# Second block of a three-block model: rope table, rope, keys' norm and values' transposes moved beside the product that makes queries, keys and values

## The reference, cut to what matters

```python
qkv = h @ w_qkv                                    # h: normed tokens, 512 x 1024
q = rope_slice(rms_norm(q, q_gain), cos, sin, 0)   # 16 heads of 64, norm per head, 16 of 64 features turned
k = rope_slice(rms_norm(k, k_gain), cos, sin, 0)   # 4 heads of 64
sc = q @ k.T * 64 ** -0.5                          # band: |query - key| <= 128
m = max(max(sc), sink)
p = exp(sc - m); p = p / (sum(p) + exp(sink - m))
o = p @ v
```

## Time and profile before

| | us |
|---|---|
| median of 3 runs (lowest, highest) | 3731.3 (3728.52, 3731.86) |
| the profiled execution's own time | 3727.72 |
| its span | 3725.9 |
| TensorE busy | 3421.0 (92%) |
| VectorE busy | 2036.8 (55%) |
| ScalarE busy | 1451.3 (39%) |
| GpSimd busy | 737.9 (20%) |

### The profile page before, as it was taken

One profiled execution on the slowest core, in us unless ns is written; L12 is line 12 of the kernel. 1 busy time (PEld: TensorE's weight loads), 2 busy tenths in 40 slices (PEclk: granted clock), 3 DMA queues, 4 the chain that ended last, 5 costly groups with the idle time before them and its releaser, 6 DMA issues. The chain is left out here.

```text
span 3725.9 us, 46521 instructions
## 1 busy us (share of the span) xinstructions
PE 3421.0 (92%) x18648; PEld 2713.6 (73%) x18648; DVE 2036.8 (55%) x2943; ACT 1451.3 (39%) x2400; POOL 737.9 (20%) x506
## 2 busy tenths in 40 slices
PE   8988999999879999977999997997999999989998
PEld 6656788877457888753688775766888888768787
DVE  6565534356555434535557375536666666546554
ACT  6435322344354222322544242445454444334232
POOL 1000302120002212201011012415444444301100
PEclk9889999999789999986999997998999999989999
DMA  4101322222012222210033232442000000022222
GB/s 145 34 1 60 105 96 96 95 80 68 1 40 85 96 94 93 96 39 0 19 107 111 74 102 71 160 163 65 21 24 24 24 24 32 4 83 96 96 91 79
DMA packets 82293, 260.48 MB, mean 70 GB/s; under 512 B 9632, under 2 KB 13216, under 8 KB 81696
## 3 DMA queue, kind: packets, MB, share of 16 engines
q1 hardware_dynamic: 71424, 236.02, 19.0%
q10 hardware_dynamic: 10656, 21.50, 1.5%
HBM read 236.51 MB, written 20.97 MB: 69 GB/s over the span
## 5 line engine op out<-in xcount | busy, mean ns | idle before, releaser
L1512 DVE TENSOR_TENSOR mlp_w_lo<-mlp_ring,mlp_w_hi 128x1024 fp32r<-128x1024 f32 (+1 forms) x211 | 251.3, 1192 | 601.4 <-ACT mlp_w_hi L1492 601.2
L1492 ACT ACTIVATE mlp_w_hi<-mlp_ring 128x1024 fp32r<-128x1024 f32 (+1 forms) x211 | 213.2, 1011 | 689.8 <-PE ps L1470 683.9
L1512 DVE TENSOR_TENSOR ffn_w_lo<-ffn_ring,ffn_w_hi 128x1024 fp32r<-128x1024 f32 (+3 forms) x172 | 222.4, 1293 | 469.8 <-ACT ffn_w_hi L1492 469.8
L1492 ACT ACTIVATE ffn_w_hi<-ffn_ring 128x1024 fp32r<-128x1024 f32 (+3 forms) x172 | 187.3, 1089 | 509.9 <-PE ps L1470 504.9
L1469 PE MATMUL ps<-mlp_more_parts,mlp_w_hi 128*128 128x512 f32 x952 | 374.0, 393 | 0.0
L1468 PE MATMUL ps<-mlp_more_parts,mlp_w_hi 128*128 128x512 f32 x760 | 306.5, 403 | 38.4 <-DVE mlp_w_lo L1512 24.1
L1468 PE MATMUL ps<-tiles_parts,mlp_w_hi 128*128 128x512 f32 x832 | 331.0, 398 | 5.7 <-issue 5.7
L1468 PE MATMUL ps<-ffn_x_parts,ffn_w_hi 128*128 128x512 f32 x792 | 312.3, 394 | 22.7 <-DVE ffn_x_parts L2202 20.9
L1470 PE MATMUL ps<-tiles_parts,mlp_w_lo 128*128 128x512 f32 x832 | 328.7, 395 | 0.0
L1469 PE MATMUL ps<-ffn_x_parts,ffn_w_hi 128*128 128x512 f32 x792 | 310.1, 392 | 0.0
L1470 PE MATMUL ps<-ffn_x_parts,ffn_w_lo 128*128 128x512 f32 x792 | 309.9, 391 | 0.0
(11 more groups left out here) (486 smaller groups left out, 7057.7 us busy)
## 6 DMA issues: line engine op xcount, KB each, us to landing
ffn_ring<-in_w_ffn_up SPq DMA_DIRECT2D x88, 512.0 KB, 3.3
mlp_ring<-in_w_up SPq DMA_DIRECT2D x64, 512.0 KB, 3.3
mlp_ring<-in_w_down SPq DMA_DIRECT2D x64, 512.0 KB, 3.3
rwkv_keep<-ffn_ring ACTq DMA_DIRECT2D x64, 256.0 KB, 2.3
sq<-rwkv_keep SPq DMA_DIRECT2D x64, 256.0 KB, 2.9
ffn_ring<-in_w_ffn_down SPq DMA_DIRECT2D x16, 768.0 KB, 4.3
in_ring<-in_w_in SPq DMA_DIRECT2D x22, 512.0 KB, 3.3
mlp_ring<-in_w_in SPq DMA_DIRECT2D x22, 512.0 KB, 3.3
```

The source lines that it names most:

```text
L1492: nc.scalar.activation(w.w_hi[:, n % SPLIT, 0:width], w.ring[:, n % RING, 0:width], ACT.Copy).then_inc(s["w_hi_ready"], 1)
L1512: nc.vector.tensor_tensor(w.w_lo[:, n % SPLIT, 0:width], w.ring[:, n % RING, 0:width], w.w_hi[:, n % SPLIT, 0:width].bitcast(F32), ALU.sub ...
```

## The change

The stages of `second_block` before the attention go. Their work is done in a new class, `Attended`, whose programs are woven into the last two products of the `mlp1` chain: the rope table's 12 VectorE steps beside the gate's tiles 4, 5 and 6; rope of keys and queries, the keys' norm, the doubled keys and the values' transposes beside and behind the 12 tiles of the product. The product's tile order becomes keys (0, 1), queries (2 to 9), values (10, 11). The queries are not normed: the rotation uses a matrix that is multiplied with the gain, and the queries' rstd per token and head goes into the exponential's scale and into the maximum, by one more instruction per group. The chain `mlp1` uses 5 banks for output tiles, so that bank 5 is free for the sums of squares. GpSimd has no part in it any more. The positions and the bands are loaded by SP within the chain, behind the load for gate tile 4, after a wait for all slots before the gate; SP then waits until the bands have landed.

```diff
+def qkv_product(nc, m, a, normed, y, prep):
+    def on_dve(dve, s, lin, t):
+        if t == 0:
+            normed.invert(dve, s)
+        if t < lin.tiles:
+            dve.wait_ge(s["slots_used"], lin.used(t))
+            nc.vector.tensor_tensor(y[:, t, :], m.ps[:, lin.bank(t), :], m.rstd[:], ALU.mult).then_inc(s["bank_free"][lin.bank(t)], 1)
+        prep.beside("dve", dve, s, t if t < lin.tiles else math.inf)
+    def on_act(act, s, lin, t):
+        if t == 0:
+            normed.root(act, s)
+        prep.beside("act", act, s, t if t < lin.tiles else math.inf)
+    def beside(t):
+        def emit(pe, s):
+            if t == 0:
+                normed.sums(pe, s)
+            prep.beside("pe", pe, s, t if t < QKV_TILES - 1 else math.inf)
+        return emit
...
@@ gated_embedding, on_dve @@
+        if prep and t < DT:
+            prep.beside("dve", dve, s, t - DT)
@@ class Attended @@
+    def tables_in(self, a, gate):
+        def emit(sp, s):
+            sp.wait_ge(s["slots_used"], gate.slot)
+            sp.dma_start(self.positions, a["positions2"]).then_inc(s["q_positions_in"], 16)
+            sp.dma_start(self.bands, a["bands2"]).then_inc(s["q_bands_in"], 16)
+            sp.wait_ge(s["q_bands_in"], 16)
+        return emit
+    def act(self, act, s):
+        yield 0
+        act.wait_ge(s["r_angles"], 1)
+        for t in (m.sin, m.cos):
+            nc.scalar.activation(t[:], t[:], ACT.Sin).then_inc(s["r_tables"], 1)
+        for n in range(10):
+            yield n + 1
+            self.there(act, s, n)
...
+            nc.scalar.activation(into, tile, ACT.Square).then_inc(s["b_squared"], 1)
+            if n == 3:
+                act.wait_ge(s["b_k_sums"], 1)
+                nc.scalar.activation(self.k_root, m.ps[:, 7, 0:4 * NT], ACT.Sqrt, ...).then_inc(s["b_k_root"], 1)
+            if n == 6:
+                act.wait_ge(s["b_k_turned"], 1)
+                nc.scalar.activation(self.k_rows, m.ps[0:4, 7, :], ACT.Copy).then_inc(s["b_k_rows"], 1)
+        yield 12
+        act.wait_ge(s["b_sums"], 8)
+        nc.scalar.activation(self.root, m.ps[:, 5, 0:16 * NT], ACT.Sqrt, ...).then_inc(s["b_root"], 1)
+        for g in range(2):
+            act.wait_ge(s["b_v_turned"], g + 1)
+            nc.scalar.activation(self.v_tok[:, g, ...], m.ps[:, 6 + g, :], ACT.Copy).then_inc(s["b_v_ready"], 1)
+    def pe(self, pe, s):
+        for beat in range(1, 12):
+            yield beat
+            n = beat - 1
+            if n < 10:
+                self.there(pe, s, n)
+                if n == 0:
+                    pe.wait_ge(s["b_ready"], 3)
+                else:
+                    pe.wait_ge(s["b_sine"], n)
...
+                nc.tensor.matmul(m.ps[:, 6, :], rot, tile, start=True, stop=True).then_inc(s["b_rotated"], 1)
+            if beat == 3:
+                pe.wait_ge(s["b_squared"], 2)
...             # 8 matmuls of keys' squares, 2 columns each, into bank 7 -> b_k_sums
+            if beat == 6:
+                pe.wait_ge(s["b_k_rstd"], 1)
...             # 4 transposes of 4 columns into bank 7 -> b_k_turned
+            if beat in (8, 10):
+                g = (beat - 8) // 2
+                if g == 0:
+                    pe.wait_ge(s["b_k_rows"], 1)
+                else:
+                    pe.wait_ge(s["b_doubled"], 4)
+                nc.tensor.matmul(m.ps[:, 7, :], m.rows_out[0:4, g * P:(g + 1) * P], self.k_rows, ...).then_inc(s["b_spread"], 1)
+            if beat >= 4:
+                i = beat - 4
+                pe.wait_ge(s["b_squared"], i + 3)
...             # 4 matmuls of a query tile's squares, 2 columns each, into bank 5 -> b_sums
+        for g in range(2):
+            self.there(pe, s, QV + g)
+            if g == 0:
+                pe.wait_ge(s["b_sine"], 10)
+            else:
+                pe.wait_ge(s["b_doubled"], 8)
...         # 4 transposes of a value tile into bank 6 + g -> b_v_turned
+    def dve(self, dve, s):
+        yield -DT
...     # rotation matrices times gains, negative sinks -> b_ready
+        yield -4
+        dve.wait_ge(s["q_positions_in"], 16)
+        next(angles)                       # 3 steps
+        yield -3
+        next(angles)                       # 5 steps
+        yield -2
+        next(angles)                       # 4 steps
+        dve.sem_inc(s["r_angles"], 1)
+        for n in range(10):
+            yield n + 1
+            self.there(dve, s, n)
+            nc.vector.scalar_tensor_tensor(out=self.cosine[:, n % 2, :], in0=tile, scalar=gain, in1=m.cos[:], ...)
+            dve.wait_ge(s["b_rotated"], n + 1)
+            nc.vector.tensor_tensor(self.sine[:, n % 2, :], m.ps[:, 6, :], m.sin[:], ALU.mult).then_inc(s["b_sine"], 1)
...
+            nc.vector.tensor_tensor(tile, self.cosine[:, n % 2, :], self.sine[:, n % 2, :], ALU.add).then_inc(s["b_roped"], 1)
+            if n == 4:
+                yield 5.5
+                dve.wait_ge(s["b_k_root"], 1)
+                nc.vector.reciprocal(self.k_root, self.k_root).then_inc(s["b_k_rstd"], 1)
+            if n >= 8:
+                g = n - 8
+                yield 9.2 + 2 * g
+                dve.wait_ge(s["b_spread"], g + 1)
...             # 4 products of 64x512, keys times bank 7, into the doubled keys -> b_doubled
+        yield 12
+        dve.wait_ge(s["b_root"], 1)
+        nc.vector.reciprocal(self.root, self.root).then_inc(s["b_rstd"], 1)
...     # two scalings of 128x64: POS_Q and NEG_Q
@@ band_attention @@
-                    nc.vector.scalar_tensor_tensor(out=st(n, NEG_MAX), in0=st(n, MAX), scalar=-HD ** -0.5, in1=by_bank(neg_sink, n), ...)
+                    nc.vector.tensor_tensor(st(n, SCALED_MAX), st(n, MAX), scale_of(NEG_Q, n), ALU.mult)
+                    dve.wait_ge(s["scaled_max"], n + 1)
+                    nc.vector.tensor_tensor(st(n, NEG_MAX), st(n, SCALED_MAX), by_bank(f.neg_sink, n), ALU.min)
-                            nc.scalar.activation(p[...], scores_of(n)[:, y, slot, :], ACT.Exp, scale=HD ** -0.5, ...)
+                            nc.scalar.activation(p[...], scores_of(n)[:, y, slot, :], ACT.Exp, scale=scale_of(POS_Q, n)[:, y, slot:slot + 1], ...)
```

More of the change, by code:

```diff
@@ L175, in rope_table @@
     magic = 12582912.0
[L176 to L212, removed]
@@ new lines, in rope_angles @@
+    for part in (high, mid, low):
+        step(nc.vector.scalar_tensor_tensor(out=sin[:], in0=turns, scalar=-part, in1=sin[:], op0=ALU.mult, op1=ALU.add))
+    yield
+    step(nc.vector.tensor_scalar(turns, sin[:], np.pi / 2, -two_pi, ALU.is_gt, ALU.mult))
+    step(nc.vector.scalar_tensor_tensor(out=cos[:], in0=sin[:], scalar=np.pi / 2, in1=turns, op0=ALU.add, op1=ALU.add))
+    for t in (sin, cos):
+        step(nc.vector.tensor_scalar(t[:], t[:], 3.1415925, -3.1415925, ALU.min, ALU.max))
+    yield
@@ L314, in by_bank, with scale_of @@
             return columns[:, g * 8 + h:g * 8 + h + G].rearrange("p (s y) -> p y s", y=2)
+        def scale_of(which, n):
+            return by_bank(f.scales[:, which, groups[n][2], :], n)
         def st(n, which):
@@ L523, in dve @@
     def dve(self, dve, s):
[L524 to L530 removed]
+        nc, m = self.nc, self.m
         done = [0]
@@ L1418, in chain @@
     for lin in linears:
-        lin.slot = len(slots)
+        lin.slot, lin.banks = len(slots), banks
         for t in range(lin.tiles):
@@ L1438, in steps @@
                     yield lin, lin.tiles + more
-    with stage(nc, name, f"loaded*{RING}", "w_hi_ready", "w_lo_ready", "slots_used", "small_done", f"bank_free*{BANKS}", *signals) as (block, s):
+    with stage(nc, name, f"loaded*{RING}", "w_hi_ready", "w_lo_ready", "slots_used", "small_done", f"bank_free*{banks}", *signals) as (block, s):
         @block.sync
@@ L1457, in _ @@
                 tile = lin.place[t]
-                if part == 0 and tile >= BANKS:
-                    pe.wait_ge(s["bank_free"][tile % BANKS], tile // BANKS)
+                if part == 0 and tile >= banks:
+                    pe.wait_ge(s["bank_free"][tile % banks], tile // banks)
                 pe.wait_ge(s["w_lo_ready"], n + 1)
-                into = m.ps[:, tile % BANKS, :]
+                into = m.ps[:, tile % banks, :]
                 for k in range(lin.ks):
@@ L1772, in dve, with gated_embedding @@
                                                 op0=ALU.mult, op1=ALU.mult).then_inc(s["post_scaled"], 1)
-def gated_embedding(nc, m, a, layer, normed, e, then):
+def gated_embedding(nc, m, a, layer, normed, e, then, prep=None):
     sq = m.sq
@@ L1850, in in_projection @@
     return [first, Linear(a["w_in"], layer * NIN, NIN, DT, normed.rhs, normed.arrived, 1, {t: beside(t) for t in range(NIN)}, act, dve, last=2)]
-def scaled_product(nc, m, weights, tiles, normed, y):
+def qkv_product(nc, m, a, normed, y, prep):
     def on_dve(dve, s, lin, t):
```

257 lines of the change are left out of this document (128 added, 129 removed).

## The result

The changed kernel took 3677.3 us, the median of four executions (3675.3 to 3681.6), against 3731.2 for the kernel before in the same job (3728.5 to 3731.9): a ratio of 0.9866, 95% interval 0.9852 to 0.9881. The forecast was 3679, range 3667 to 3692.

A forecast was written before the change was run, and what follows sets the result against it. TensorE, busy 92% of the span, was taken as the bound. Terms -84.2 + 19.4 + 4.6 + 3.0 + 3.3 + 1.6 = -52.3 us, from a median of 3731.3, gave 3679 us, range 3667 to 3692.

The forecast's parts named there:

- removed, net: Between the second block's product and its attention: 90.6 us of stages go, 6.4 us stay, 84.2 us saved.
- TensorE work in the product: Inside the product: rotations, sums of squares, transposes and spreads put between the tiles' matmuls add 19.4 us.
- two waits: In the product, TensorE idles behind tiles 6 and 10 waiting for VectorE, 2.3 us each, 4.6 us; bounds 0 and 8.
- clock behind them: In the product, matmuls after each idle time run at the low clock: 1.5 us each, 3.0 us; bounds 0 and 4.
- angles beside the gate: At the gate's last tiles, rope-table steps put VectorE behind and delay normed tiles: 3.3 us; bounds 0 and 8.
- attention: In attention, one more small peak instruction costs 0.2 us in eight groups: 1.6 us; bounds -3 and 6.4.
- the product (28.5 for 25 to 28): Sign: from first tile's end to last tile's end the product grows by 25 to 28 us.
- the barrier (1.14 for at most 1): Sign at the attention stage's start: a barrier with more than 1 us would show the prediction wrong; 0.82 was counted.
- angles collide: Rival: at gate tiles 5 and 6 GpSimd and VectorE hold each other up, 8 us instead of 3.3; 3684; chance 0.12.
- Stage's start: From the end of the product's last matmul to the first score's matmul: 6.4 us, with four doubled products at 2.6.
- the banks: Five banks instead of six in the second layer's chain cost nothing; rival that they make it slower than before, chance 0.02.
- SP's two DMAs: Before the load of gate tile 5, SP's two loads and its wait cost nothing, as loads are issued 22 us ahead.

The follow-up runs named there:

- waits gone: Kernel after with the keys' roots inverted one step earlier and both spreads and the doubled keys one beat earlier: 3670.7 us, ratio 0.9846 to the kernel before.

## Why the prediction was right, and where its terms were not

The steps as the prediction put them, with what the stretch shows (after less before, us):

```
step                            forecast   measured   from
removed, net                     -84.2      -83.4     E-S 90.64 and 7.25
TensorE work in the product      +19.4      +19.8     gaps behind tiles 1 to 10, waits gone
two waits                         +4.6       +5.0     2.36 and 2.66
clock behind them                 +3.0       +3.7     the rest of T1-E: 28.5 - 19.8 - 5.0
angles beside the gate            +3.3       +5.5     N-T1, 36.51 and 30.97
attention                         +1.6       +2.4     S-O (2.8 between the means)
sum                              -52.3      -47.0     N-F
```

The mechanism held at every step, and the two large terms, 84.2 removed and 19.4 added, came out within 0.8 us, because both were read from rows of the same work elsewhere in the trace. The sum was 5.3 us too good, and all six terms erred to that side. That the medians nevertheless fell by 53.9 us in the first job (and by 49.2 in the second) is the 3420 to 3432 us of unchanged code: before's median alone was 3723.1 to 3731.2 over the jobs. With the measured steps the prediction's own sum would have given 3731.3 - 47.0 = 3684. That 3679 stood so near 3677.3 is luck. Two of the prediction's signs came out beyond their bounds, as told above: the product (28.5 for 25 to 28) and the barrier (1.14 for at most 1).

**Angles (3.3, measured 5.5).** The step took the collision as a wash: "perhaps two" steps meet GpSimd and the tail saves as much. By the rows above more met it: L1580 took 2.20 instead of 1.23, L185 1.50 instead of 0.43, L186 1.63 instead of 0.69, and the three of L183 3.12 instead of 2.14, 4.0 us in all against the 3.0 that the tail saved. The Trainium skill (SBUF — State Buffer, "Who interferes with whom") says that a VectorE instruction with two SBUF inputs, or in a two-port mode, contends with a GpSimd one that reads SBUF, and that the shared ports are held for a whole instruction. The trace agrees with it, L185's 1.50 against 0.43. So the wash was short by 1.0, and it left out the clock behind it. 4.5 us reach the end of tile 0, and 1.0 more comes behind it, where TensorE's sums of squares ran at the low clock. The rival "angles collide" had the cause right and the size too large (8): the truth lay about half way between it and the forecast.

**Attention (1.6, measured 2.4 to 2.8).** The peak's second instruction was sized well (1.6, measured 1.8), in part by luck: in the row of waits from which it was counted only 0.9 shows (4.2 with it, 3.3 without). The failed sentence is that a scale from a table costs nothing because "the instruction stays" and ScalarE waits there anyway. It costs 1.6 us, 90 ns in each exponential, 560 and 666 against 470 and 577. ScalarE does wait, but the exponential is a link of the chain score, peak, exponential, turning, so each of the 32 groups has a chain longer by its two exponentials. TensorE waited 4.2 us for the chain's end, where it had waited 1.9. The Trainium skill (ScalarE: Activation LUTs, "What ACT_TABLE_LOAD costs") gives some 93 ns for each per-partition operand of an ACTIVATE; the trace agrees with its 90, and the price could have been had before the run. At the same clock the two cost 3.2 us. From S to O only 2.4 of it shows, because the attention of the kernel after started a little better than that of the kernel before: granted 0.60 over the first 11.5 us instead of 0.53, worth 0.8 (110.45 before against 109.65 with the same attention in the new kernel). The prediction had put that start at nothing, with a bound of 3.

**Clock (3.0, measured 3.7).** Right in size, wrong in place: 1.5 behind each wait was forecast, 0.2 and 3.2 were measured, and 0.3 are hundredths in each slot.

**Stage's start (6.4, measured 7.25)** as told beside its rows; the four doubled products took 2.83, not 2.6. It was right that nothing else stands there. Costed at nothing and rightly so: the banks, SP's two DMAs (no wait of a slot for its weights), the squares on ScalarE, and, by 1.78 in every usual gap against 1.77 forecast, VectorE's cosine, sine and sum.

**What could be had.** The waits and the angles were found by the prediction, and removing them gave 13.3 us up to the first score and 14 in the stretch, from 253.3 to 239.2: more than the 10.9 that the three terms had been given, since the second pair's doubled keys also left the start of the stage.

## To carry to other kernels

When a stage is taken off the critical path, price its pieces from rows of the same work done beside another product in the same trace: terms got that way came within 0.8 us, while terms reasoned from "it is hidden" (the collision with GpSimd, the operand of the exponential) were short by a third and more. Ask of each instruction that gets a new operand what that operand costs, also where its engine waits, if the instruction is a link in a chain. And where unchanged code drifts by 12 us, compare marks around the changed stretch, not spans; and where the clock differs at its start, compare from where it is full.

## What the runs showed of the hardware

- A scale read from a table adds 90 ns to an ACTIVATE of 256 or 384 columns (560 and 666 against 470 and 577 ns).
- TensorE's clock fell from 2.4 to 1.2 GHz with no idle time before it, behind 3 us of a rotation, a spread and two-column sums, and slots then took 6.2 to 6.4 us instead of 4.8, from first third matmul to last. In other places the same 3 us were followed by a slot at the full clock (4.80, both waits gone, behind tile 7). Within the product it falls at the same place from one execution of a kernel to the next (5.74 and 5.71; 6.41 and 6.40).
- But small shifts move it: the same idle time of 2.36 us cost 0.2 us of clock in the kernel after and 1.6 with the product 5.5 us earlier; 2.66 us cost 3.2 or 1.6. Two kernels that differ in the number of banks alone started the same attention at 0.53 and 0.82 (granted clock over 11.5 us), 1.4 us apart from S to O. What decides in these cases no run here settles.
- At the full clock the attention repeats to 0.07 us over 83.3 (eight executions), while whole executions of one kernel differ by nearly 20 us, the slower ones at a lower mean granted clock (3737.1 at 0.947, 3718.5 at 0.953).
- VectorE's instructions on 512 columns took 1.50 and 1.63 us beside GpSimd where alone they take 0.43 and 0.69.
